# A decoder step whose weights go through a ring of four single tiles instead of units of two

## The reference

```python
def hybrid_layer(x, p, attn_fn, lru_h0, lru_buf, sc_buf):
    x = x + 0.5 * swiglu(rms_norm(x, p['ffn1_norm']), p['ffn1_w_in'], p['ffn1_w_out'])   # hidden 2816
    h = rms_norm(x, p['mix_norm'])
    q, k, v, f, bx_in, by_in, sb, sc, sx, g = split_columns(h @ p['w_in'])
    q, k = rms_norm(q, p['q_norm']), rms_norm(k, p['k_norm'])          # per head, 8 heads of 64
    logf = jax.nn.log_sigmoid(f + p['b_forget'])
    o_a = attn_fn(q, k, v, logf)            # prompt: causal; samples: with 256 cached positions
    xc, lru_buf_new = causal_dwconv(bx_in, lru_buf, p['lru_conv_w'])
    hb, h_last = rg_lru(xc + p['lru_conv_b'], lru_h0, ...)
    o_b = hb * jax.nn.gelu(by_in)
    uc, sc_buf_new = causal_dwconv(sc * sx, sc_buf, p['sc_conv_w'])
    o_c = sb * uc
    merged = sum(sigmoid(g[b]) * (o[b] @ wb[b]) for b in range(3))     # o = o_a, o_b, o_c
    x = x + merged @ p['w_out']
    x = x + 0.5 * swiglu(rms_norm(x, p['ffn2_norm']), p['ffn2_w_in'], p['ffn2_w_out'])
    return x, (k, v, logf, h_last, lru_buf_new, sc_buf_new)
```

## Time and profile before

| | |
|---|---|
| time, median of 3 runs | 3120.39 us (3118.79 to 3121.61) |
| span of the profiled execution | 3121.0 us |
| PE busy | 2990.7 us (96%) |
| DVE busy | 1465.1 us (47%) |
| ACT busy | 992.6 us (32%) |
| DMA, mean share of 16 engines | 2 to 3 tenths, 80 GB/s |
| chain that ended last | PE 89%, DVE 4%, ACT 2%, issue 2% |
| weight splits, ACT L752 and DVE L1006 | 456 each, 1043 and 1206 ns |

### The profile page before, as it was taken

How to read it: one execution, slowest core, us unless ns; L and a number is a source line. 1 busy time by engine, 2 the same in 40 slices (tenths; PEclk the granted TensorE clock), 3 DMA queues, 4 the chain that set the end, 5 groups by cost and what they waited for, 6 DMA issues and landing times.

```text
span 3121.0 us, 54813 instructions
## 1 busy us (share of the span) xinstructions
PE 2990.7 (96%) x21632; PEld 2892.3 (93%) x21632; DVE 1465.1 (47%) x2025; ACT 992.6 (32%) x1287; POOL 104.4 (3%) x104
## 2 busy tenths in 40 slices
PE   7999998999999999999999999989999999999998
PEld 7999998888899999999999999988889999999998
DVE  4434345555745443343443333466565544433334
ACT  4211123444533332211231212324445333312123
POOL 1000001000000000000000000100000001000001
PEclk9999999999999999999999999999999999999999
DMA  3222222333222222222222222222332222222222
GB/s 114 79 82 81 79 64 82 83 81 81 70 87 81 85 81 80 82 67 81 69 82 68 95 68 81 81 64 79 80 81 89 80 82 88 81 68 81 81 78 74
DMA packets 299022, 248.82 MB, mean 80 GB/s; under 512 B 20643, under 2 KB 296307, under 8 KB 298919
## 3 DMA queue, kind: packets, MB, share of 16 engines
q1 hardware_dynamic: 296775, 242.44, 25.4%
q0 software_dynamic: 2144, 4.98, 0.5%
HBM read 240.04 MB, written 7.34 MB: 79 GB/s over the span
## 4 chain that ended last, share of the span: by engine, by line
PE 89%; DVE 4%; ACT 2%; issue 2%; DVEq 1%; DMA 0%; POOLq 0%; ACTq 0%; SPq 0%
PE ps L448 81%; PE ps L609 2%; PE ps L664 1%; ACT whi L752 1%; DVE wlo L1006 1%; PE ps L693 1%; PE ps L587 0%; PE ps L610 0%; DVE tmp L1012 0%; DVEq L1046 0%; PE ps L654 0%; PE ps L596 0%; ACT hh L771 0%; DVE x L1023 0%; PE ps L640 0%
## 5 line engine op out<-in xcount | busy, mean ns | idle before, releaser
L1006 DVE TENSOR_TENSOR wlo<-wraw,whi 128x1024 fp32r<-128x1024 f32 (+1 forms) x456 | 548.9, 1206 | 1351.9 <-ACT whi L752 1349.4
L448 PE MATMUL ps<-hh,whi 128*128 128x288 f32 x4480 | 968.9, 298 | 18.8 <-ACT vtok L850 6.1
L448 PE MATMUL ps<-hl,whi 128*128 128x288 f32 x4480 | 962.9, 297 | 0.0
L448 PE MATMUL ps<-hh,wlo 128*128 128x288 f32 x4480 | 961.9, 296 | 0.0
L752 ACT ACTIVATE whi<-wraw 128x1024 fp32r<-128x1024 f32 (+1 forms) x456 | 474.6, 1043 | 1460.1 <-PE ps L448 1409.0
L448 PEld LDWEIGHTS ps<-hh,whi 128*128 128x128 f32 x4480 | 725.4, 190 | 25.5 <-ACT vtok L850 6.3
L448 PEld LDWEIGHTS ps<-hl,whi 128*128 128x128 f32 x4480 | 725.7, 190 | 0.0
L448 PEld LDWEIGHTS ps<-hh,wlo 128*128 128x128 f32 x4480 | 724.9, 189 | 0.0
L448 PE MATMUL ps<-ah,whi 128*128 128x288 f32 x1408 | 313.8, 306 | 72.5 <-DVE al L1052 72.5
L448 PE MATMUL ps<-al,whi 128*128 128x288 f32 x1408 | 311.1, 304 | 0.0
L448 PE MATMUL ps<-ah,wlo 128*128 128x288 f32 x1408 | 309.8, 302 | 0.0
(11 more groups left out here) (282 smaller groups left out, 2503.5 us busy)
## 6 DMA issues: line engine op xcount, KB each, us to landing
wraw<-in_ffn_w_in SPq DMA_DIRECT2D x88, 1024.0 KB
wraw<-in_ffn_w_out SPq DMA_DIRECT2D x32, 1024.0 KB
wraw<-in_w_in SPq DMA_DIRECT2D x28, 1024.0 KB
wraw<-in_w_in SPq DMA_DIRECT2D x56, 512.0 KB
wraw<-in_ffn_w_out SPq DMA_DIRECT2D x16, 768.0 KB
wraw<-in_w_branch SPq DMA_DIRECT2D x24, 512.0 KB
wraw<-in_w_out SPq DMA_DIRECT2D x9, 1024.0 KB
kv<-in_cache_k SPq DMA_DIRECT2D x128, 64.0 KB, 1.9
```

Of the source, the lines that this page charges most:

```text
L448: last = pe.matmul(ps[slot][:, half, 0:HF], weights, rhs[:, k, half * HF:(half + 1) * HF], start=(start and c == 0 and n == 0), stop=(stop ...
L1006: dve.tensor_tensor(split_tile(wlo, j, rowwise), raw_tile(slot, j, rowwise), split_tile(whi, j, rowwise).bitcast(F32), ALU.subtract).then_ ...
```

## The change

`wraw` becomes a ring of four slots of one tile (RING = 4), and `whi` and `wlo` have four slots too. `wlo` takes the same memory as `wraw`: VectorE writes the low half over the raw numbers. Every tile has a load of its own, 512 KB in pieces of 512 bytes (256 KB where only 4 chunks are wanted), with one semaphore for each slot. Tiles are split three ahead: at K(k) ScalarE splits W(w+3). A load may go to a slot only when TensorE has left it, which is told by the split of the tile before: the load of W(n) waits for `hi_ready` of W(n-1). In the parts with 6 chunks the load takes 8 rows of chunks, and TensorE skips two. In `merge` the branch tiles are split as 4 chunks, but for one in each step. In `fv` the first split stands at K0 on both engines, and SP waits for K2 ahead of the pairs. VectorE gets a drain ahead of reading K20.

```diff
-    def unit(self, k, layer, step=0):
-        return layer * self.plan["layer_units"] + step * self.units + self.first_unit + k
+    def weight(self, w, layer, step=0):
+
+        return (layer * self.plan["layer_units"] + step * self.units) * 2 + (self.first_unit * 2 + w)
...
-        wraw = sb("wraw", [P, 2, KD * 256])
-        whi = sb("whi", [P, 2, KD * P], F32R)
-        wlo = sb("wlo", [P, 2, KD * P], F32R)
+        with ExitStack() as m:
+            wraw = sb("wraw", [P, RING, KD * P], F32, m)
+        wlo = sb("wlo", [P, RING, KD * P], F32R)
+        whi = sb("whi", [P, RING, KD * P], F32R)
...
+        def ahead(st, w):
+
+            w2 = w + AHEAD
+            if st is S["pair"] and w2 in (6, 7) or st is S["merge"] and w2 in (3, 6, 7, 10, 11):
+                return w2 % RING, 4
+            return w2 % RING, KD
...
-                sp.wait_ge(lo_ready, n * 2 - 2 + AHEAD)
...
+                sp.wait_ge(hi_ready, st.weight(w, L, i) + 1)
+                src = t_in[name].rearrange("l (k p) n -> l p k n", p=P)[bass.ds(L, 1), :, k0:k0 + kc, bass.ds(c0, P)]
+                dst = wraw[:, w % RING, 0:kc * P].rearrange("p (k c) -> p k c", c=P)
+                sp.dma_start(dst, src.rearrange("l p k n -> p (l k) n")).then_inc(tile_loaded[w % RING], 16)
...
+                        for w in range(4):
+                            load(st_out, w, L, i, w2, done - (KD - kc), KD, i * 512 + P * w)
...
+                wait_apart(sp, filled[fv.slot(2)], fv.turn(2, L) + 1)
...
-                    load(pr, 0, L, p, ("w_in", 0, KD, p * P + COL_Q, P), ("w_in", 0, KD, p * P + COL_K, P))
-                    load(pr, 1, L, p, ("w_in", 0, KD, p * P + COL_BX, P), ("w_in", 0, KD, p * P + COL_BY, P))
-                    load(pr, 2, L, p, ("w_in", 0, KD, p * P + COL_SC, P), ("w_in", 0, KD, p * P + COL_SX, P))
+                    for w, col in enumerate((COL_Q, COL_K, COL_BX, COL_BY, COL_SC, COL_SX)):
+                        load(pr, w, L, p, "w_in", 0, KD, p * P + col)
...
-                    load(pr, 3, L, p, ("w_in", 0, KD, p * P + COL_SB, P))
+                    for w in (6, 7):
+                        load(pr, w, L, p, "w_in", (w - 6) * 4, 4, p * P + COL_SB)
...
-                u, j, rowwise = ahead(st, w)
-
-                base = st.first_unit + u
-                slot = base % 2
-                act.wait_ge(unit_loaded[slot], L * (plan["layer_units"] // 2 * 32) + i * (st.units // 2 * 32) + (base // 2 + 1) * 32)
-                act.activation(split_tile(whi, j, rowwise), raw_tile(slot, j, rowwise), ACT.Copy).then_inc(hi_ready, 1)
+                slot, chunks = ahead(st, w)
+                act.wait_ge(tile_loaded[slot], st.ring_turn(w + AHEAD, L, i) * 16 + 16)
+                act.activation(part(whi, slot, chunks), part(wraw, slot, chunks), ACT.Copy).then_inc(hi_ready, 1)
...
+                split_ahead(fv, 0, 0, L)
                 act.wait_ge(absz_ready, L + 1)
                 act.activation(tmp[3][0:F_W, 0:N], tmp[2][0:F_W, 0:N], ACT.Exp, scale=-1.0).then_inc(expz_ready, 1)
-                split_ahead(fv, 0, 2, L)
                 split_ahead(fv, 1, 2, L)
...
-                dve.wait_ge(hi_ready, st.unit(0, L, i) * 2 + (w + 3))
+                dve.wait_ge(hi_ready, st.weight(w + AHEAD, L, i) + 2)
```

More of the change, by code:

```diff
@@ L283, in two, with part @@
             return ap.rearrange("p (b n) -> p b n", b=2)
[L285 to L300, removed]
+        def part(buf, slot, chunks):
+            return buf[:, slot, 0:chunks * P]
+        def ahead(st, w):
[3 more added lines that the diff above has]
+            return w2 % RING, KD
         block = ctx.enter_context(nc.Block())
@@ L375, in _ @@
                 fv = S["fv"]
-                for k in range(2):
-                    load(fv, k, L, 0, ("w_in", 0, KD, COL_V + 256 * k, 256))
+                for w in range(4):
+                    load(fv, w, L, 0, "w_in", 0, KD, COL_V + P * w)
                 pr = S["pair"]
+                wait_apart(sp, filled[fv.slot(2)], fv.turn(2, L) + 1)
                 with sp.Fori(0, PAIRS) as p:
@@ L404, in _ @@
                     for b in range(3):
[L405 to L406 removed]
+                        for w in range(2):
+                            load(mg, 4 * b + w, L, i, "w_in", 0, KD, i * 256 + (COL_G + D * b + P * w))
+                        for w in range(2):
+                            whole = b == 0 and w == 0
+                            load(mg, 4 * b + 2 + w, L, i, "w_branch", 4 * b, KD if whole else 4, i * 256 + P * w)
                 with sp.Fori(0, 2) as i:
[L408 to L409 removed]
+                    for w in range(4):
+                        load(S["out"], w, L, i, "w_out", 0, KD, i * 512 + P * w)
                 ffn("ffn2", L)
[L412 to L414 removed]
+            for w in range(AHEAD):
+                sp.wait_ge(hi_ready, 2 * DEPTH * plan["layer_units"] + w + 1)
+                sp.dma_start(wraw[:, w, :], t_in["w_out"][0, 0:P, :]).then_inc(tile_loaded[w], 16)
             post = DEPTH * plan["layer_tiles"] + PRE_TILES
@@ L436, in wait_weights, with project @@
             def wait_weights(st, w, L, i=0):
-                pe.wait_ge(lo_ready, st.unit(0, L, i) * 2 + (w + 1 + AHEAD))
-            def project(slot, w, chunks, rhs_hi, rhs_lo, start=True, stop=True, before=None):
+                pe.wait_ge(lo_ready, st.weight(w, L, i) + 1)
+            def project(slot, w, chunks, rhs_hi, rhs_lo, start=True, stop=True, before=None, skip=0):
                 for c, k in enumerate(chunks):
@@ L450, in project, with plain @@
                 return last
-            def plain(st, k, w, chunks, rhs_hi, rhs_lo, L, i=0, before=None):
+            def plain(st, k, w, chunks, rhs_hi, rhs_lo, L, i=0, before=None, skip=0):
                 wait_weights(st, w, L, i)
                 wait_psum(st, k, L, i)
-                project(st.slot(k), w, chunks, rhs_hi, rhs_lo, before=before).then_inc(filled[st.slot(k)], 1)
+                project(st.slot(k), w, chunks, rhs_hi, rhs_lo, before=before, skip=skip).then_inc(filled[st.slot(k)], 1)
             def norm(st, n, L):
@@ L486, in ffn @@
                         for k in range(4):
[L487 removed]
+                            plain(st_out, k, k, range(kc), ah, al, L, i, skip=KD - kc)
             pe.wait_ge(x_loaded, X_LOADS * 16)
@@ L818, in _ @@
                 act.activation(hh[:, c, :], x[:, c, :], ACT.Copy, scale=gains[:, 0, c:c + 1]).then_inc(hh_ready, 1)
-            first_weights(1)
+            for j in range(1, AHEAD):
+                first_weights(j)
             act.wait_ge(pre_done, 2)
```

62 lines of the change are left out of this document (22 added, 40 removed).

## The result

| | before | after |
|---|---|---|
| median | 3121.0 us (3118.8 to 3122.3) | 3292.7 us (3283.0 to 3296.1) |
| span of the profiled execution | 3121.0 us | 3290.1 us |
| mean granted clock of TensorE | 0.978 | 0.946 |

The ratio is 1.0545 (95% interval 1.0533 to 1.0558). The change costs 172 us; the forecast was +103, with an upper end of 3285. The direction and the places were right, and the size was not.

The account below looks back on a forecast made before the run. TensorE, busy 96% of the span, was taken as the bound, so only its waits count. Pairs +107, values -10, forget gates +4, merge +2 gave +103 on 3120.4: 3223 us, range 3172 to 3285.

Parts of the forecast that it names:

- eight pairs: Head pairs: pages and weight loads queue behind one another, each pair 13.4 us longer, +107 us in all.
- values stage: `values(1)` loses its 5.8 us wait and the low clock behind it, the second split waits 3.3 us: -10 us.
- cached forget gates: First part of ffn1: 16 loads of 18.35 us delay the next part's W0; +4 us for two layers.
- merge: Branch tiles last 3.2 us against a turn of 4.5, mostly given back by gate tiles: +2 us for two layers.
- the paragraph on the granted clock in the pair: Wait for `kv` may halve the clock in the 16 transposes, adding 1.8 us; 13.4 taken between 12.4 and 14.2.
- if the low clock holds through the query-key products too: Upper end for the head pairs: 18 us a pair, 144 us in all.
- W8's forecast wait: The next pair's W0, loaded behind the `cache_v` pages, lands at 63.5; ScalarE wants it at 60.2, waits 3.3 us.
- The load's time: Weight loads: 3.2 us for 512 KB, from issue to end of traffic; 2.4 us taken for 256 KB.
- margin of 0.3 us: Last feed-forward part: a load-and-split turn of 4.5 us against about 4.8 a tile on TensorE, so it keeps pace.
- rival A: Weight loads bound everywhere; last feed-forward parts' turn 5.5 against 4.8, 22 us more: 3245, up to 3285; chance 0.14.
- Rival B: Head pairs: one of two ScalarE waits falls away, 8 us a pair, +60 us: 3180; chance 0.15.
- the 12 waits for `al`: Feed-forward hand-overs to the second matmul: waits of about 6 us stay, costing and gaining 0.

Follow-up runs that it names:

- both gaps filled: Changed kernel plus unread matmuls on TensorE, 38 ahead of the cached keys' transposes and 20 ahead of the query-key products: 3265.5 us, ratio 1.0459.
- the first gap filled: Changed kernel plus only the 38 unread matmuls ahead of the transposes of the cached keys, where TensorE waits for `kv`: 3292.8 us, ratio 1.056.
- the old kernel with late pages: Kernel before, without the ring, with SP waiting for K1 of this pair ahead of `wab` and the `cache_k` pages: 3198.8 us, ratio 1.0271.
- The split behind the copies: Changed kernel with key pages and the next pair's first load spread in SP's order, plus second splits moved behind the `probt` and `vtok` copies: 3131.1 us.
- the second gap filled: Changed kernel plus only the 20 unread matmuls ahead of the query-key products, where TensorE waits for ScalarE's copy: 3271.5 us, ratio 1.0484.

## Why the prediction was wrong in size

The spans differ by 169.1 us. Taken from the two traces by stage, for both layers:

| term | forecast | measured |
|---|---|---|
| eight pairs | +107 | +152 (76.3 and 75.6, 19.0 a pair) |
| values stage | -10 | -2 |
| cached forget gates | +4 | +8.4 |
| merge | +2 | +5.7 |
| start | below 1 less | -1.8 |
| the rest: last feed-forward parts, `out`, end | 0 | +7 |

**The step that failed** is the paragraph on the granted clock in the pair. It let the clock fall for the transposes only, at most 1.8 us, took 13.4 between 12.4 and 14.2, and kept "if the low clock holds through the query-key products too" as the upper end, 18 a pair. That end, for which it gave no working, is what happens. The two waits stood in the forecast side by side, 4.2 us for `kv` and then K10 held up for ScalarE's copy behind the split of W7; what it didn't ask is what each does to the clock of the work right behind it. Behind them stand the query-key products, which ran at half clock until shortly before K14 in all eight pairs: 16.6 us for 9.5, in the pair shown 7.8 us more, of which 3.3 are taken out of W8's forecast wait. With both gaps filled the stretch is 9.5 us again. Either wait can do it: ScalarE's copies alone did in the eight pairs of the kernel with the first gap filled, the pages alone in two pairs of the old kernel with late pages.

By the sum: 12.4, and 1.8 for K10 (0.9 for a later issue of `wab`, 1.0 for two loads of 2.9 us for 2.4), and 7.8 - 3.3 for the products, and 0.6 for W2's load of 3.8 us for 3.2, give about 19.3; the pair at 722.50 took 19.6 more. Part of the 0.9 is the clock as well: behind the wait for `probt` it is at 0.50 in 722 to 724, and K0 fills 7.4 us into the pair for 6.8; then the split of W4 waits 1.4 us for its load. The 1.8 us of the slow transposes, the only clock term taken, isn't in it: TensorE would have waited for W7's split instead. The first gap's experiment shows this too.

**The load's time** was read at the end of its traffic, 3.2 us, and the semaphore comes later. In this trace the load at 760.40 moved its last bytes between 762.5 and 763.0, and ScalarE's split began at 763.34. The Trainium skill (DMA: Bandwidth & Descriptors, Anatomy of one DMA) says that most of the fixed part is the receipt of the last byte. Its fit gives 3.2 us for 512 KB and 2.6 for 256 KB; the measured 3.8 and 2.9 decide, and the fit is of the other kind of queue. This is also why the last feed-forward part fell short of its margin of 0.3 us. ScalarE's splits there, in the changed kernel:

```profile
460.77 1.06 ACT L750 ACTIVATE whi<-wraw 128x1024 fp32r<-128x1024 f32 x1 [0.46 <-DMA wraw<-in_ffn_w_out]
465.79 1.06 ACT L750 ACTIVATE whi<-wraw 128x1024 fp32r<-128x1024 f32 x1 [0.47 <-DMA wraw<-in_ffn_w_out]
470.90 1.06 ACT L750 ACTIVATE whi<-wraw 128x1024 fp32r<-128x1024 f32 x1 [0.57 <-DMA wraw<-in_ffn_w_out]
```

The idle time is put down to the load each time, and the turn is 5.07 us where TensorE needs 4.8. That was rival A's mechanism, with a price of some 2 us a part and not 5.5. It is likely part of the 7 us of the rest (TensorE's wait for `hl` behind the last part is 5.1 us in two, and was 1.6), though no experiment took it apart; loads of 6 chunks in place of 8, which would shorten the turn, were not tried.

**The values stage** went by the right reading and a wrong size. The 5.8 us wait went, but of the two splits behind `values(1)` the second waits for its load: it starts at 530.89, after 4.47 us of waiting for 3.3 forecast, and the `vtok` copies begin at 531.85.

```profile
525.36 1.06 ACT L750 ACTIVATE whi<-wraw 128x1024 fp32r<-128x1024 f32 x1 [7.36 <-PE ps L548]
530.89 1.06 ACT L750 ACTIVATE whi<-wraw 128x1024 fp32r<-128x1024 f32 x1 [4.47 <-DMA wraw<-in_w_in]
531.85 1.91 ACT L849 ACTIVATE vtok<-ps,small 128x256 f32<-128x256 f32 x5
```

From the first matmul of `values(0)` TensorE asks for its slot after 30.6 us, where it was 39.1; that is the forecast's 5.8 and 2.9. It pays 4.5 us back here, with a wait of 7.5 us for 3.1. Another 3.2 us go ahead of `values(0)`: the forget product there waits 2.5 us for `hl`, for 0.8, and then runs at half clock (0.50 in 493 to 495). The split behind the copies brought the wait for `vtok` down to 2.0 us.

**The cached forget gates** cost twice the forecast, in part for the same reason. In the first layer TensorE waits 2.4 us for `wlo` at 198.03, for 1.9 forecast, and the clock, for which this sum had no term, is at 0.50 from 199 to 201.

**Right** were: the wait for `kv`, 4.7 us in the mean for 4.2; the path through W6 and W7 to K10 (45.8 us into the pair for 44.0); the wait for the `probt` copies; the 12 waits for `al`, unchanged; `values(1)` without its wait. The `wab` loads, with the pages behind them, go out 15.8 us after the pair's start for 14.9. Rival B, with half of the delays hidden, was nearer than it looks: W8's wait did vanish, but because something worse stood ahead of it.

## What to carry to other kernels

A queue that issues everything in one order turns any new wait into a wait for all that stands behind it: when single buffers replace a pair, move the other loads among the weight loads, and put a split that must wait for its load behind copies that needn't. When a wait is forecast for TensorE, look at what runs right behind it, and price that at half clock. It was half for 16 to 17 us of query-key products behind a wait of 2.0 us (the kernel with the first gap filled), and for some 4.5 us of full tiles behind one of 6.0. Take a load's time from issue to its waiter's start, not to the end of its traffic. And when a gap is filled to test what it does to the clock, look at the clock ahead of the work in question: with the second gap filled it was back before the products began, and that test could clear no wait.

## What was not expected of the hardware

Behind the two waits of a pair the clock stayed at half through 16 to 17 us in which TensorE was never idle: query-key products with 64 rows and the samples' small ones behind them. It came back in the last 2 us ahead of K14 or as K14 began. In the pair shown that is between 785 and 786; in the first pair it is at 0.83 in 594 to 595, and K14 starts at 596.13. With the same products entered at full clock and without a wait it stayed at 1.00 throughout, in all eight pairs of the kernel before and of the one with both gaps filled. In one pair with the first gap filled it fell only some 2 us after K10 had begun: K10 is at 2206.28, the clock is 1.00 in 2206 to 2208 and 0.54 in 2208 to 2210.

The clock can fall without any wait. In the kernel before, in the pair of the earlier trace rows, TensorE goes from 32 small matmuls (128 by 16) straight into the last `weighted` at 679.99, and its clock is at half in it:

```profile
679.00:680.00 1.00, 1.00 (x10) 0.97 (x10) 0.85 (x5) 0.00 (x0) 0.00 (x0) 1.00 0.07 6
681.00:682.00 1.00, 1.00 (x3) 0.43 (x2) 0.93 (x2) 0.00 (x0) 0.00 (x0) 0.50 1.14 345
```

The Trainium skill (TensorE: Matmul & The Clock Gate, Part 1: The HAM clock gate) says that the clock's level follows how busy the array has lately been. TensorE had work for 2.00 of 2.00 us at either level here, so its busy time in the windows doesn't tell the level. Why the products hold a level that they can't regain isn't shown by these runs.

Between the last traffic of a load and the start of what waits for it lie 0.3 to 0.8 us in the one load taken apart above, and a load of 256 KB takes 2.9 us against 3.8 for 512 KB: half of the bytes save only a quarter of the time.
